# Two-layer hybrid trunk on one core: inverse square roots by logarithm and exponential, and the decode rows' chain spread over the output products

## What is computed

```python
h = rms_norm(x, p['pre_g'])
proj = jnp.einsum('bsd,de->bse', h, p['w_in'])            # 14 column groups
conv_out, conv_buf_new = short_conv(c_b, c_c, c_x, conv_buf, p['conv_w'])
rwkv_out, shift_new, rwkv_state_new = rwkv7_mix(r_sh, shift_prev, rwkv_state, p)
q = rms_norm(q_down, p['q_norm_g']) @ w_uq;  ckv = rms_norm(ckv_raw, p['kv_norm_g'])
krope = rope(kr_raw, pos)                                  # latent attention with a rotary key
o_lat = attend(q_lat, q_rope, ckv, krope)                  # causal (prompt) or over the cache (decode)
mem_out = mem_attend(mem_q, mem_k, mem_v)                  # 256 memory tokens
mixed = concat([conv_out * silu(c_gate), rwkv_out * silu(r_gate), mla_out * silu(..), mem_out * silu(..)])
x = x + rms_norm(mixed @ w_out, p['post_g'])
```

## Time and profile before

| | |
|---|---|
| time, median of 3 runs | 3907.51 us (3903.33 to 3907.8) |
| the profiled execution's own time | 3909.04 us |
| its span, first to last instruction | 3907.2 us |
| mean granted TensorE clock | 0.972 |
| PE busy | 3648.7 us (93%) |
| DVE busy | 1853.7 us (47%) |
| ACT busy | 1377.5 us (35%) |
| POOL busy | 145.5 us (4%) |

### The profile page before, as it was taken

One profiled execution on the slowest core, in us unless ns is written; L12 is line 12 of the kernel. 1 busy time (PEld: TensorE's weight loads), 2 busy tenths in 40 slices (PEclk: granted clock), 3 DMA queues, 4 the chain that ended last, 5 costly groups with the idle time before them and its releaser, 6 DMA issues.

```text
span 3907.2 us, 74485 instructions
## 1 busy us (share of the span) xinstructions
PE 3648.7 (93%) x30760; PEld 2657.1 (68%) x30760; DVE 1853.7 (47%) x4403; ACT 1377.5 (35%) x3739; POOL 145.5 (4%) x278
## 2 busy tenths in 40 slices
PE   4988999999999999999879789999999999999997
PEld 3755777676767677586547477777767687776763
DVE  2544635454544535455325445353645455364542
ACT  1332333434342433534323324333343434334351
POOL 0000000000000000000000000000000000000000
PEclk8998999999999999999889899999999999999998
DMA  6323243333324142241433242524233341522313
GB/s 223 122 92 117 89 154 100 122 99 119 124 87 155 57 150 90 86 126 41 147 124 100 66 138 68 175 79 165 89 122 100 104 137 46 172 81 99 101 39 115
DMA packets 319405, 431.82 MB, mean 111 GB/s; under 512 B 26670, under 2 KB 276460, under 8 KB 318908
## 3 DMA queue, kind: packets, MB, share of 16 engines
q1 hardware_dynamic: 292348, 375.00, 29.4%
q0 software_dynamic: 11648, 41.95, 3.1%
q10 hardware_dynamic: 15072, 10.10, 0.9%
HBM read 405.22 MB, written 32.26 MB: 112 GB/s over the span
## 4 chain that ended last, share of the span: by engine, by line
PE 81%; DVE 7%; ACT 5%; DVEq 3%; issue 3%; DMA 1%; ACTq 0%; POOL 0%; SPq 0%; POOLq 0%
PE bank L669 74%; PE bank L673 7%; DVEq L1306 3%; DVE T L1410 1%; DVE ml L1668 1%; ACT Q L2205 0%; ACT Sm L2280 0%; ACT PT L2320 0%; ACT qr L2204 0%; ACT mix L2176 0%; DVE xin L1738 0%; DVE T L1422 0%; DVE T L1420 0%; DVE pr L1418 0%; DVE T L1413 0%
## 5 line engine op out<-in xcount | busy, mean ns | idle before, releaser
L669 PE MATMUL bank<-hT,win 128*128 128x256 f32 (+3 forms) x6912 | 1636.0, 387 | 5.9 <-ACT hT L2030 4.5
L669 PEld LDWEIGHTS bank<-hT,win 128*128 128x128 f32 (+1 forms) x6912 | 1268.5, 189 | 238.8 <-issue 40.6
L669 PE MATMUL bank<-kv,Q 96*128 96x512 f32 (+3 forms) x640 | 278.3, 533 | 11.0 <-ACT mix L2045 11.0
L1668 DVE TENSOR_REDUCE ml<-bank 128x1 f32<-128x512 f32 (+3 forms) x320 | 195.3, 610 | 131.1 <-PE bank L669 120.5
L673 PEld LDWEIGHTS bank<-cst,Sm 128*128 128x128 f32 x1344 | 154.0, 141 | 141.8 <-issue 66.5
L673 PE MATMUL bank<-cst,Sm 128*128 128x128 f32 x1344 | 215.8, 282 | 27.2 <-ACT Sm L2280 19.4
L2280 ACT ACTIVATE Sm<-bank,ml 128x512 f32<-128x512 f32 (+3 forms) x320 | 200.0, 625 | 80.9 <-DVE ml L1673 72.1
L669 PE MATMUL bank<-wout,mix 128*128 128x512 f32 x512 | 225.5, 593 | 1.6 <-DVE mix L1718 1.6
L1727 DVE TENSOR_TENSOR st<-st 128x1 f32<-128x1 f32 (+1 forms) x34 | 5.4, 158 | 426.7 <-ACT mix L2176 425.5
L669 PEld LDWEIGHTS bank<-wout,mix 128*128 128x128 f32 x512 | 96.0, 190 | 116.8 <-issue 114.6
L2045 ACT ACTIVATE mix<-bank 128x256 f32<-128x256 f32 x128 | 49.2, 384 | 328.1 <-PE bank L669 328.1
(11 more groups left out here) (446 smaller groups left out, 5919.7 us busy)
## 6 DMA issues: line engine op xcount, KB each, us to landing
win<-in_w_in SPq DMA_DIRECT2D x176, 1024.0 KB, 5.3
wout<-in_w_out SPq DMA_DIRECT2D x68, 512.0 KB, 7.6
xin<-out_xres SPq DMA_DIRECT2D x32, 1024.0 KB, 7.7
PT<-in_w_out SPq DMA_DIRECT2D x32, 512.0 KB, 4.4
XX<-in_w_out SPq DMA_DIRECT2D x32, 512.0 KB, 4.1
out_xres<-xin SPq DMA_DIRECT2D x16, 1024.0 KB
win<-in_w_in SPq DMA_DIRECT2D x16, 896.0 KB, 4.9
win<-in_w_in SPq DMA_DIRECT2D x16, 640.0 KB, 4.5
```

The source lines that it names most:

```text
L669: return pe.matmul(out, lhsT, rhs, start=start, stop=stop, skip_group_check=True)
L1668: v.tensor_reduce(top, bank[:, 0:w], AX, MAX)
```

## The change

- The whole-tile inverse roots become `exp(-0.5 * ln(x))`, both on ACT. DVE's three wide reciprocals per block go.
- The chain of the decode rows no longer stands after block 0. Its steps stand between the output products of blocks 0 to 4 (`sample_step` on PE; `sample_latents`, `sample_prepare`, `sample_states`, `sample_finish` on DVE ahead of `residual`; `sample_queries` and `sample_gates` on ACT ahead of `finish`). It works in banks 0 to 2 and in parts of `kv` that the prompt has not filled yet. DVE signals when it has read these banks (`s_sbk`), and PE waits for that at the start of blocks 1 to 5.
- In every block that turns rows for a next one, step 1 of `project_out` waits for `hT`'s first half.
- Tile 8 is made as two halves of 128 tokens into the lower and upper 64 partitions of its bank; ACT takes them with four copies instead of two.
- The stores of the decode rows are issued by SP, POOL's gathers 3 and 4 of block 0 wait for the same signal as in the other blocks, three small rotary-table loads per layer are added, and one `memset` of `kv` at the start is gone.

```diff
+                    memory_rows(B.unit + 1 if B.block else l * NS, B.it)
                     if B.block == 0:
-                        B = Block(l, None)
-                        rope_rows(B)
-                        sp.wait_ge(s_mo.h, s_mo.at(l * NB, 1))
+                        sp.wait_ge(s_mem["kvr"].h, s_mem["kvr"].at(l, 1))
                         for b in range(NS):
-                            sp.dma_start(S0[:, 2 * b:2 * b + 2, :],
+                            sp.dma_start(S0[b // 4][:, 2 * (b % 4):2 * (b % 4) + 2, :],
                                          a["state_rwkv"][sl, b].rearrange("a (p h) i j -> (h i) (a p) j", p=2)).then_inc(s_sl.h, 16)
-                        memory_rows(l * NS, B.it)
-                    else:
-                        memory_rows(B.unit + 1, B.it)
+                    sample_stores(B.block)
...
+                if f == 64:
+                    for k in range(KD):
+                        for j in range(2):
+                            n = P + j * B.ns
+                            last = mm(PP[bank][64 * j:64 * j + 64, 0:n], win[:, g % 2, k, c:c + 64], hT[:, k, j * P:j * P + n], k == 0, k == KD - 1)
+                    last.then_inc(s_pj.h, 1)
+                    return
...
+                if 1 <= B.block <= 5:
+                    pe.wait_ge(s_sbk.h, s_sbk.at(B.l, B.block))
...
+            def sample_step(B, i0):
+
+                l = B.l
+                if i0 == 1 and B.turns:
+                    pe.wait_ge(s_hT.h, s_hT.at(B.px + 1, 1))
+                if B.block == 0:
+                    if i0 == 1:
+                        pe.wait_ge(s_sdv.h, s_sdv.at(l, SDV["squares"]))
+                        mm(PP[0][:, 0:NS], ones, ssq[:, 0, :])
+                        mm(PP[0][:, NS:2 * NS], ones, ssq[:, 1, :], True, False)
+                        mm(PP[0][:, NS:2 * NS], ones, ssq[:, 2, :], False, True).then_inc(s_spe.h, 1)
+                    elif i0 == 3:
+                        pe.wait_ge(s_sdv.h, s_sdv.at(l, SDV["normed"]))
+                        for h in range(NH):
+                            for t in range(2):
+                                mm(PP[1][:, h * NS:(h + 1) * NS], wuq[:, t, h, :], sqd[:, t, :], t == 0, t == 1)
+                        tr(PP[1][0:NS, P:2 * P], sck[:, :], P)
+                        tr(PP[1][0:NS, 2 * P:2 * P + RD], skrr, RD).then_inc(s_spe.h, 1)
+                    elif i0 == 5:
+                        pe.wait_ge(s_sac.h, s_sac.at(l, SAC["queries"]))
+                        for h in range(NH):
+                            last = mm(PP[0][:, h * NS:(h + 1) * NS], wukT[:, h, :], sQ96[:, h, :])
+                        last.then_inc(s_spe.h, 1)
...
+                elif B.block in (2, 3):
+                    i = (i0 // 2 - 1 if i0 % 2 == 0 else -1) + (3 if B.block == 3 else 0)
+                    if i0 in (2, 4) or i0 == 6 and B.block == 2:
+                        pe.wait_ge(s_sdv.h, s_sdv.at(l, SDV["spread"] + i))
+                        for q in range(2):
+                            last = mm(PP[q][:, :], bones, e4[q])
+                        last.then_inc(s_spe.h, 1)
...
+                elif B.block == 4:
+                    if i0 == 1:
+                        mm(PP[0][:, 0:2 * NS], bones, syy).then_inc(s_spe.h, 1)
...
-                    if B.block == 0:
-                        B = Block(l, None)
-                        sample_begin(B)
-                        sample_rwkv(l)
-                        group_norm(B, 0)
-                        group_norm(B, 1)
-                        sample_queries(l)
...
                 v.wait_ge(s_rd.h, s_rd.at(it, 1))
-                v.reciprocal(t2, t2)
-                v.reciprocal(sqn[:, 0:2, 0:n], sqn[:, 0:2, 0:n])
-                drain()
                 v.tensor_tensor(t1, t1, t2, MULT)
...
                 v.wait_ge(s_rd.h, s_rd.at(B.it, 2))
-                v.reciprocal(t, t)
-                drain()
                 v.tensor_tensor(y, y, t, MULT)
...
+                    if B.block == 0:
+                        sample_latents(B)
+                    elif B.block == 1:
+                        sample_prepare(B)
+                    elif B.block == 2:
+                        sample_states(l, (0, 1, 2))
+                    elif B.block == 3:
+                        sample_states(l, (3, 4))
+                    elif B.block == 4:
+                        sample_finish(l)
+                    if B.block < 5:
+                        drain()
+                        v.tensor_copy(st[:, 47:48], st[:, 46:47]).then_inc(s_sbk.h, 1)
                     residual(B)
-                    if B.block == 0:
-                        B = Block(l, None)
...
                     act.wait_ge(s_rw.h, s_rw.at(it, 1))
-                    act.activation(T2[:, :, 0:n], T2[:, :, 0:n], ACT.Sqrt)
-                    act.activation(sqn[:, 0:2, 0:n], sqn[:, 0:2, 0:n], ACT.Sqrt).then_inc(s_rd.h, 1)
+                    act.activation(T2[:, :, :], T2[:, :, :], ACT.Ln)
+                    act.activation(sqn[:, 0:2, :], sqn[:, 0:2, :], ACT.Ln)
+                    act.drain()
+                    act.activation(T2[:, :, :], T2[:, :, :], ACT.Exp, scale=-0.5)
+                    act.activation(sqn[:, 0:2, :], sqn[:, 0:2, :], ACT.Exp, scale=-0.5).then_inc(s_rd.h, 1)
...
                     act.wait_ge(s_rw.h, s_rw.at(B.it, 2))
-                    act.activation(T1[:, :, 0:B.n], T1[:, :, 0:B.n], ACT.Sqrt).then_inc(s_rd.h, 1)
+                    act.activation(T1[:, :, :], T1[:, :, :], ACT.Ln)
+                    act.drain()
+                    act.activation(T1[:, :, :], T1[:, :, :], ACT.Exp, scale=-0.5).then_inc(s_rd.h, 1)
...
+                    if B.block == 0:
+                        sample_queries()
+                    elif B.block == 1:
+                        sample_gates()
                     finish(B)
...
-                    if B.block:
-                        pool.wait_ge(s_mo.h, s_mo.at(B.ip, 1))
-                        gather(B.block, 3)
-                        gather(B.block, 4)
+                    pool.wait_ge(s_mo.h, s_mo.at(B.ip, 1))
+                    gather(B.block, 3)
+                    gather(B.block, 4)
+                    step = {0: SDV["roots"], 1: SDV["key_roots"], 4: SDV["variance"]}
+                    if B.block in step:
+                        pool.wait_ge(s_sdv.h, s_sdv.at(l, step[B.block]))
+                        pool.tensor_tensor(sinv, sinv, mhalf[:, :].unsqueeze(2).broadcast_to([P, 2, NS]), POW).then_inc(s_spo.h, 1)
                     out_roots(B)
-                    if B.block == 0:
-                        pool.wait_ge(s_sts.h, s_sts.at(l, s_sts.n))
```

More of the change, by code:

```diff
@@ L77 @@
 NCONST = _o
+SPE = dict(norms=1, queries=2, latent=3, own=4, keys=5, lora=6, bonus=7, spread=8, mean=13, variance=14, turned=15)
+SDV = dict(squares=1, roots=2, normed=3, rotated=4, own=5, shifted=6, keys=7, key_roots=8, decay=9, bonus=10, spread=11, out=16,
+           centred=17, variance=18)
+SAC = dict(queries=1, latent=2, tanh=3, lora=4, decay=5)
 def loads_of_slot(g):
@@ L1369, in rwkv_prepare @@
                 shift(B, 6, 7, 1)
-                if B.prompt and B.block:
+                if B.block:
                     decode_operands(B.unit)
@@ new lines, in spread @@
+            def spread(l, i):
+                vec3 = [seP, sT1, sB, spr[:, 2:4, :], spr[:, 0:2, :]][i]
+                for q in range(2):
+                    for a_ in range(2):
+                        o = e4[q].rearrange("p (b a j) -> p b a j", b=4, a=2)[:, :, a_, :]
+                        last = v.tensor_tensor(o, vec3[:, a_, 4 * q:4 * q + 4].unsqueeze(2).broadcast_to([P, 4, 64]),
+                                               K("id64").unsqueeze(1).broadcast_to([P, 4, 64]), MULT)
+                last.then_inc(s_sdv.h, 1)
@@ L1764, in sample_rwkv, with sample_states @@
+            def sample_states(l, steps):
+                if steps[0] == 0:
+                    v.wait_ge(s_sac.h, s_sac.at(l, SAC["decay"]))
+                    v.wait_ge(s_sl.h, s_sl.at(l, s_sl.n))
+                for i in steps:
+                    spread(l, i)
+                    v.wait_ge(s_spe.h, s_spe.at(l, SPE["spread"] + i))
                     for q in range(2):
-                        rows = PP[2 * (i % 2) + q][:, :].rearrange("p (a j) -> p a j", j=64)
-                        s_ = S0[:, 8 * q:8 * q + 8, :]
@@ L2062, in take @@
                                 o = dst[name][:, i, 0:n]
[L2063 to L2070 removed]
+                            take_tile(B, t, o)
+                            if B.block:
+                                decode(B.unit, t)
                     def halves(bank, m, parts=P):
@@ L2078, in begin @@
                     take("wlal")
-                    if not (B.prompt and B.block):
+                    if not B.block:
                         tanh()
                     take("k")
-                    if B.prompt and B.block:
+                    if B.block:
                         tanh()
```

(20 more changed lines are left out.)

513 lines of the change are left out of this document (247 added, 266 removed).

## The result

The changed kernel takes 3780.84 us (median of 4 runs, 3779.04 to 3782.65), beside 3905.42 us (3902.12 to 3907.80) of the kernel before on the same chip. The ratio is 0.9682, 95% interval 0.9665 to 0.9698. The profiled execution took 3779.04 us with a span of 3777.2, against 3909.04 and 3907.2. I had said 3787, range 3766 to 3817.

The account below looks back on a forecast made before the run. PE was taken as the bound. From the profiled 3909.04 us, 170.0 came off and 50.2 went on, leaving 3789.2; with the median 1.5 below the profiled execution, the forecast was 3787, range 3766 to 3817.

Parts of the forecast that it names:

- The chain goes from behind block 0: Behind block 0 in both layers: the decode rows' nearly empty stretches on PE go entirely, 124.9 us saved.
- Slow restart: First four tiles of block 1: without the idle stretch PE's clock does not fall, 1.8 + 2.0 = 3.8 us saved.
- Products of the steps: Between output products of blocks 0 to 4: PE gets the decode products back, 17 us per layer, 34 us added.
- Waits at step 1: Step 1 of project_out: PE waits for hT, in block 0 also DVE's squares; 12 x 1.0 + 2 x 2.1 = 16.2 us added.
- Tile 8: Tile 8 in 16 blocks: products into alternating partition halves overlap, 1.74 x 16 = 27.8 us saved.
- Roots at the start: Block starts: KR comes earlier, so PE's idle time before the product needing it goes, 13.5 us saved.
- The other steps at nothing: Decode steps other than step 1: each hidden behind the output products, costed at nothing.
- A clock of 1.00 in the output products: Output products: PE's clock stays 1.00; anything below was named as a sign the prediction was wrong.
- the halves of tile 8 do not overlap: Tile 8: halves sharing weight columns gain nothing, 28 us more, 3815; chance 0.08.
- the second load is dearer: ACT before step 1: second table load costs one more load's length at 14 places, 18 us, 3805; chance 0.12.
- the steps wait for each other: About 17 cross-engine steps a layer, little room in blocks 0 and 1: 1 us each, 34 us, 3821; chance 0.08.
- The slower rival: Step 1's pause halves PE's clock for the seven steps left in 14 blocks: 336 us, 4123; chance 0.03.

Follow-up runs that it names:

- the combined kernel: Changed kernel with the logarithm/exponential set hand-loaded except in block 1, hT wait at step 2 in block 1, block 0's decode squares earlier on DVE: 3763.39 us.
- the first experiment: Changed kernel with tile 8 whole again, one tile of 64 columns over all 256 tokens, and ACT's two copies: 3806.97 us.
- the long pause: Changed kernel with the end root taken twice over on ACT, two table loads and two activations more before hT: 3865.47 us.

## Why the prediction was right, point by point

The forecast was 3787, the median 3780.84. The profiled span fell by 130.0 where the sum had 119.8. The medians fell by 124.6 only, since here the profiled execution of the kernel before stands 3.6 us above its median and that of the changed kernel 1.8 below.

- **The chain goes from behind block 0.** Said 124.9. Right: the tails before were 89.69 and 92.01, where the bare output products take 28.37, that is 125.0.
- **Slow restart.** Said 3.8. Right: of the first tiles' slow start 1.77 went in layer 0 and 2.02 in layer 1. The body of block 1 in layer 0 gained 2.0 more, for which I had no term. Of this 1.5 stands at the tile before which PE waited 1.35 us for weights, at full clock; another 0.35 stands at a wait for DVE in the recurrence. Why these waits are gone is not shown.
- **Products of the steps.** Said 34. Measured 32.8: 5.2 in block 0 (33.55 in the combined kernel less 28.37), 1.2, 5.15, 3.43 and 1.43 in blocks 1 to 4, that is 16.4 a layer. Doubling them confirms the sizes in blocks 1 to 4; in block 0 only a third of the short products was doubled (1.48).
- **Waits at step 1.** Said 12 x 1.0 + 2 x 2.1 = 16.2. Measured 12 x 0.89 + 2 x 2.06 = 14.8. The second load starts 0.05 us behind the logarithm (448.36 after 448.31); I had allowed 0.08 and let `take_h` start 0.1 after the exponential, while the two overlap by 0.09.
- **Tile 8.** Said 27.8, measured 16 x 1.70 = 27.2.
- **Roots at the start.** Said 13.5, measured 14 x 1.06 + 2 x 0.63 = 16.1 (in the blocks 0 PE had idled 0.47 us only). This is the term most off. The mechanism is right, and the size lacked what surrounds a pause: the product behind it lasts 0.33 instead of 0.27, and PE's queue starts again without overlap, 0.17 a block.
- **The other steps at nothing.** Right: no idle time stands at steps 2 to 7 in the changed kernel.
- **A clock of 1.00 in the output products.** Wrong: one of my signs of being wrong did appear. In steps 0 and 1 of layer 0's block 0 the clock was 0.86, and the step behind the pause took 1.7 us too long. I had priced a pause at its own length and had no term for the step behind it.

Off by terms: 125.0 + 3.8 + 27.2 + 16.1 = 172.1. On: 32.8 + 14.8 = 47.6, and 1.7 for the slow step in block 0 that I did not have. 172.1 - 49.3 = 122.8, which is 3.0 more than my sum. The other 7.2 of the 130.0 stand in places for which I had no term. The ends of the layers give 2.6 and the start takes 0.8. The waits in block 1 of layer 0 give 2.0. The body of block 7 in layer 0 gives 1.9, where the kernel before had a slow stretch (clock 0.57 from 1813 to 1817). Block 4 of layer 1 gives 0.7, where PE had waited 0.67 us for ACT's `PT`. A slow stretch in the changed kernel, in block 0 of layer 1, takes 1.5. The last 2.3 are differences below 1 us in a block. These are differences between two single traces, and no experiment of mine bears on them; that they are small beside the range that I gave is luck, not foresight.

**The rivals.** That the halves of tile 8 do not overlap falls by the first experiment. That the second load is dearer falls: all loads take 1.28. The Trainium skill's page "ScalarE: Activation LUTs" (What ACT_TABLE_LOAD costs) has a drain of about 1380 ns with every switch; the trace does not agree, with 0.05 us between the logarithm's end and the load and 0.01 between the load and the exponential. The page's other rule (Table sets: the hidden batching unit), that logarithm and exponential share one set, holds on this chip: with that set loaded by hand there is one load for both, 3765.78. I had given it 14 us, by the wait at step 1 in 14 blocks; it was 12 by blocks. That the steps wait for each other is right at one step only: in block 0 step 1 waited for DVE, which I had in the sum. The slower rival, seven steps at the lower clock, falls by the long pause: one step is slow. But its first half was right, a pause can lower the clock, and I had given it no price of its own.

## What to carry to other kernels

A chain of small steps on other engines can go between large products for much less than the empty stretch that it leaves, if each step's inputs are ready before its product comes: here 125 us of empty stretch became 33 us of products and 15 of waits. Price a stall of the bound engine a little above its idle time: 0.65 us of it cost 0.89, and 0.89 cost 1.06. Behind a stall of 2.3 us or more, allow for a slow step as well; here there was one in every case. When work moves from one engine to another, ask for each place where it stands which of the two is late there: the same pair of activations was worth 1.44 us in block 1 and cost 0.89 in block 5.
